# Sparse and latent attention in one decoder layer: the first attention's units taken in a staggered order of row tiles

## The chip, the cores and the metric
The kernel runs on one core of a Trainium2 chip. The metric is the device time of one execution in microseconds (us); the kernel before takes 309.70 us, the median of 3 runs (309.48 to 309.84).

## What is computed
One decoder layer on x (512 tokens, 1024 wide, float32). One input projection feeds two causal attentions of 8 heads each, A and B.

    h = x @ w_in
    A: score = sum over 8 index heads of iw * relu(iq . ik), causal
       each query keeps its 128 best keys; softmax(q . k / 8) over them, times v
       o_a = that * silu(ga)
    B: q, k, v from low-rank latents; rotary part shared by the heads
       o_b = softmax((qn . kn + qp . kp) / sqrt(96), causal) . v * silu(gb)
    out = concat(o_a, o_b) @ w_out
    x = LayerNorm(2**0.25 * x + out)

In A the kernel does not gather keys: a bias tile holds 0 for a chosen key and a very large negative number for another, and the row softmax runs over all the keys that the causal mask leaves.

## The kernel before
**Tiles.** The 512 rows of queries are four row tiles m = 0 to 3 of 128 rows. A row tile m attends to (m+1)*128 keys, so tile 3 works on 512 columns and tile 0 on 128. P is 128, TT is 4, HEADS is 8.

**Stages.** First come seven groups of input projections (L1067), the index scores and the choice of keys beside them on VectorE, then the projections of the latents (L1067 again), then attention A, then attention B with the output projection (L1348) and the layer norm between its units, then the last row tile's output projection and norm.

**Units.** Both attentions are one list of 64 units, 32 for A and 32 for B. A unit is one head of one row tile. `unit(u)` gives for unit u its pass v (v = u // 8), its row tile m = ORDER[v % 4] with ORDER = [3, 2, 1, 0], its head h and its columns N. So A is now worked as 8 units of tile 3, 8 of tile 2, 8 of tile 1 and 8 of tile 0, and B starts again with tile 3.

**One unit of A, across the engines.** Here and below s(u), T(u) and PV(u) are the three parts of unit u on TensorE (PE):

- s(u), `scores`, L1216 and L1219: two products of 128 rows x N columns into one of two score banks. It waits until VectorE has read that bank, that is until the mask of unit u-2 is done (`masked_ready`).
- mask(u), `mask_unit` on VectorE (DVE), L887: adds the bias, scales, writes `probs` (4 buffers) and the row's extreme.
- exp(u), `exp_unit` on ScalarE (ACT), L611: the exponentials in place, and their sum into a column of `row_sum`.
- T(u), `transposes`, L1275: m+1 transposes of 128x128 into one of two banks. It waits for exp(u), and for the copy of unit u-2 out of the same bank.
- copy(u), `copy_probsT` on ACT, L631: the transposed block from that bank into `probsT`.
- PV(u), `outputs`, L1291: m+1 products, each shown in the trace as two instructions, into one half of `ps_o`; pass v uses half v % 2. It waits for copy(u).

**The order by hand.** Each engine's program is written out. PE's iteration u does s(u), then T(u-2) (T_LAG = 2), then PV(u-4) (PV_LAG = 4), then whatever is hung on that iteration. DVE's iteration u does mask(u), ACT's does copy(u-2) and then exp(u). The queues are in order.

    for u in range(NU + PV_LAG):
        if 2 <= u < NU:
            scores(u)
        if 0 <= u - T_LAG < NU:
            transposes(u - T_LAG)
        if u - PV_LAG >= 0:
            outputs(u - PV_LAG)
        if u == PET_AT:
            qpe_transposes()
        ...

**Hung on these iterations** (fixed numbers, not changed): PE transposes 8 blocks of B's rotary queries in iteration 8 (`qpe_transposes`, L1242; PET_AT = 8) and 4 of its rotary key in iteration 14 (L1249). ACT and DVE each copy four parts of the former, one an iteration, in iterations 9 to 12 (`evac_qpeT`, L603 on ACT, L872 on DVE); ACT copies the latter in 15 (L685) and splits one tile of B's values in 20 (L655). In iteration 24 (O_FIRST + T_LAG) the finished output of tile 3 is transposed (`o_transposes`, L1320), in the same pair of banks as the T blocks, and leaves it through ACT (L645) and then DVE (L919); T(24) comes next in that bank. ACT splits three more tiles of values in iterations 32 and 33, DVE takes their low parts in 33, and the output projection of tile 3 starts in iteration 34.

**End of a pass.** `normalise(v)` on DVE (L903, L904) waits until pass v's last PV is done, takes the reciprocals of 8 columns of `row_sum` and scales the output into `o_norm`; `apply_gate(v)` (L913) multiplies by the gate. They stand in DVE's iterations 4 and 5 of the next pass: 12 and 13, 20 and 21, 28 and 29, 36 and 37. PV's first unit of pass v+2 waits for the normalising of pass v.

**Beside A**, GpSimd (POOL) converts the output weights (L444, L448). SyncE starts loading the second half of those weights and others when the last scores of A are done (L351).

Of the kernel before, what the change touches and what calls it, by code (L numbers as in the profile page):

```python
# [8 lines left out]
TT = SEQ // P  # L9
KT = D_MODEL // P  # L10
A_HEADS, A_DIM = 8, 64
A_WIDTH = A_HEADS * A_DIM
# [15 lines left out]
def build(nc, x, xT, positions, freqs, w_in, q_norm_g, w_uq, kv_norm_g, w_ukv, w_out, ln_g, ln_b, out):  # L28
# [37 lines left out]
    ORDER = [3, 2, 1, 0]  # L66
    HEADS = A_HEADS
    NU_A = TT * HEADS
    NU = 2 * NU_A
    NPASS = 2 * TT  # L70
    NPAIR = TT * B_HEADS // 2

    def unit(u):
        v, h = divmod(u, HEADS)
        m = ORDER[v % TT]
        return v, m, h, (m + 1) * P


    O_AFTER = [[NU_A + HEADS * (i + 1) + OT_AT - T_LAG + b for b in range(2)] for i in range(TT - 1)] + [[NU, NU]]
# [98 lines left out]
    def col(n):  # L178
        nonlocal at
        at += n  # L180
        return small[:, at - n:at]
# [5 lines left out]
    neg_max, row_sum, rinv = col(8), col(NU), col(HEADS)  # L187
# [3 lines left out]
    with ExitStack() as ctx:  # L191
# [4 lines left out]
        def sem(name):  # L196
            return ctx.enter_context(nc.semaphore(name))
# [30 lines left out]
        scores_ready, masked_ready, probs_ready = sem("scores_ready"), sem("masked_ready"), sem("probs_ready")  # L228
        transposed, probsT_copied = sem("transposed"), sem("probsT_copied")
        pv_done = sem("pv_done")  # L230
# [4 lines left out]
        o_ps_read, o_ready = sem("o_ps_read"), sem("o_ready")  # L235
# [39 lines left out]
        def wait_tok(eng, g, m):  # L275

            eng.wait_ge(acc_read[m], 2 * (g + 1))
# [204 lines left out]
        def _(act):  # L482
# [125 lines left out]
            def exp_unit(u):  # L608
                N = unit(u)[3]
                act.wait_ge(masked_ready, u + 1)  # L610
                act.activation(probs[:, u % NPROBS, 0:N], probs[:, u % NPROBS, 0:N], ACT.Exp, bias=neg_max[:, u % 8:u % 8 + 1],  # L611
                               scale=-1.0, accum_out=row_sum[:, u:u + 1]).then_inc(probs_ready, 1)

            for first, dst in ((A_QN, qbT), (A_KN, kbT)):
                for p in range(4):
# [50 lines left out]
            for u in range(NU + T_LAG):  # L666
                if u >= T_LAG:
                    copy_probsT(u - T_LAG)
                i, j = divmod(u - NU_A, HEADS)
# [30 lines left out]
        def _(dve):  # L700
# [8 lines left out]
            def after(ins):  # L709
                dve.wait_ge(dve_step, step(ins))  # L710
# [106 lines left out]
            for i in range((TT - 1) * IDX_HEADS):  # L817
                m, h = 1 + i // IDX_HEADS, i % IDX_HEADS
                N = (m + 1) * P
# [39 lines left out]
            for first, dst in ((F_QT, qaT), (F_KT, kaT)):  # L859
                for h in range(A_HEADS):  # L860
                    n, a = first + h // 2, h % 2
# [6 lines left out]
            def evac_qpeT(j):  # L868

                quad, r = divmod(j, 2)  # L870
                dve.wait_ge(acc_ready, A_END + quad + 1)
                ins = V.tensor_copy(qbT[NOPE:B_QK, 4 * quad + 2 + r, :], ps_y[64 + 32 * r:96 + 32 * r, quad])  # L872
                if r == 1:
                    ins.then_inc(acc_read[2 + quad], 1)


            def mask_unit(u):
                v, m, h, N = unit(u)
                a = v < TT
                bias = spans[m - 1] if a and m > 0 else causal[:, SEQ - N:SEQ]  # L880
                scale = (A_DIM if a else B_QK) ** -0.5
                dve.wait_ge(scores_ready, u + 1)
                if u == 0:
                    dve.wait_ge(bias_ready, 1)
                if u >= NPROBS:
                    dve.wait_ge(transposed, slot_of[u - NPROBS] + 1)
                V.tensor_tensor_reduce(out=probs[:, u % NPROBS, 0:N], in0=ps_s[:, u % 2, 0:N], in1=bias, scale=-scale,  # L887
                                       scalar=3.0e38, op0=ALU.add, op1=ALU.min,
                                       accum_out=neg_max[:, u % 8:u % 8 + 1]).then_inc(masked_ready, 1)
# [9 lines left out]

            def normalise(v):  # L900

                dve.wait_ge(pv_done, HEADS * (v + 1))
                after(V.reciprocal(rinv, row_sum[:, HEADS * v:HEADS * (v + 1)]))  # L903
                V.tensor_tensor(o_norm[:, :].rearrange("p (h d) -> p h d", h=HEADS),  # L904
                                ps_o[:, v % 2].rearrange("p (h d) -> p h d", h=HEADS),
                                rinv.unsqueeze(2).broadcast_to([P, HEADS, A_DIM]), ALU.mult).then_inc(o_ps_read, 1)

            def apply_gate(v):
                m = ORDER[v % TT]
                cols = slice(A_WIDTH * (v // TT), A_WIDTH * (v // TT + 1))  # L910
                dve.wait_ge(o_ps_read, v + 1)
                wait_tok(dve, G_GA, m)
                V.tensor_tensor(gate[:, m, cols], o_norm[:, :], gate[:, m, cols], ALU.mult).then_inc(o_ready, 1)  # L913

            def copy_oT_lo(i, b):
                dst = (oT0, oT1)[i % 2]
                dve.wait_ge(oT_hi_ready, 2 * i + b + 1)
                src = ps_pT[:, slot_of[i, b] % 2].rearrange("p (a b) -> p a b", a=4) if b == 0 else obT[:, :, :]
                V.tensor_tensor(dst[:, 1, 4 * b:4 * b + 4, :], src, dst[:, 0, 4 * b:4 * b + 4, :],  # L919
                                ALU.subtract).then_inc(oT_lo_ready, 1)  # L920
# [3 lines left out]
            def probs_low(u):  # L924
                N, w = unit(u)[3], u % 3
                dve.wait_ge(probsT_copied, u + 1)
                V.tensor_tensor(probsT_b[:, w, 1, 0:N], ps_pT[:, slot_of[u] % 2, 0:N], probsT_b[:, w, 0, 0:N],
                                ALU.subtract).then_inc(probsT_lo_ready, 1)

            def vb_low(n):  # L930
                j = VB_ORDER[n]
                dve.wait_ge(vb_hi_ready, n + 1)
                V.tensor_tensor(vb_parts[j][:, :, 1:3], vb[:, j, :].rearrange("p (q a d) -> p q a d", a=2, d=V_DIM),
                                vb_parts[j][:, :, 0:4:3], ALU.subtract).then_inc(vb_lo_dve, 1)
# [9 lines left out]
            def row_sums(v):  # L944

                dve.wait_ge(probs_ready, HEADS * (v + 1))
                if v > TT:
                    dve.wait_ge(gate_scaled, v - TT)
                V.reciprocal(rinv, row_sum[:, HEADS * v:HEADS * (v + 1)]).then_inc(rinv_ready, 1)

            def gate_obT(i):

                n = slot_of[i, 1]
                dve.wait_ge(transposed, n + 1)
                dve.wait_ge(pair_merged, 8 * (i + 1))
                V.tensor_tensor(obT[:, :, :], obT[:, :, :], ps_pT[:, n % 2].rearrange("p (a b) -> p a b", a=4),
                                ALU.mult).then_inc(obT_ready, 1)
# [42 lines left out]
            for u in range(NU):  # L1000
                if u >= 2:
                    mask_unit(u)
                if u - T_LAG >= NU_A:
                    probs_low(u - T_LAG)
                if u == NU_A + 1:
                    vb_low(1)
                    vb_low(2)
                v, j = divmod(u, HEADS)
                i = v - TT
                if 0 < v <= TT and j == PV_LAG:  # L1010
                    normalise(v - 1)
                if 0 < v <= TT and j == PV_LAG + 1:
                    apply_gate(v - 1)
                if v > TT and j == 2:
                    row_sums(v - 1)
                if 0 <= u - PET_AT - 1 < 4:
                    evac_qpeT(u - PET_AT - 1)
                if u == O_FIRST + T_LAG:
                    copy_oT_lo(0, 0)
                if 1 < i and j == OT_AT:  # L1020
                    copy_oT_lo(i - 1, 0)
                if 0 < i and j == OT_AT + 1:
                    gate_obT(i - 1)
                if 0 < i and j == OT_AT + 2:
                    copy_oT_lo(i - 1, 1)
                if u in PAIR_AT:
                    read_pair(PAIR_AT[u])
                if u - 1 in PAIR_AT and PAIR_AT[u - 1] < POOL_PAIRS:
                    merge_pair(V, PAIR_AT[u - 1])
                for t in range(TT - 2):  # L1030
                    for at_u, take in ln_schedule(t):
                        if at_u == u:
                            take()
# [27 lines left out]
        def _(pe):  # L1061
# [133 lines left out]
            for p in range(4):  # L1195
                pe.wait_ge(acc_read[p], seen(A_QN + p))
                for t in range(QL_T):
                    s, cols = (C_UQN + t) % RING, slice(p * P, (p + 1) * P)
# [32 lines left out]
            for p in range(4):  # L1231
                pe.wait_ge(acc_read[p], seen(A_KN + p))
                s, cols = C_UKN % RING, slice(p * P, (p + 1) * P)
# [77 lines left out]
            def o_transposes(i, b):  # L1311

                m = ORDER[i]
                bank = slot(slot_of[i, b])
                if b == 0:
                    pe.wait_ge(o_ready, i + 1)
                else:
                    pe.wait_ge(gate_scaled, i + 1)
                for j in range(4):
                    ins = nc.tensor.transpose(bank[:, j * P:(j + 1) * P], gate[:, m, (4 * b + j) * P:(4 * b + j + 1) * P], ident[:, :])  # L1320
                ins.then_inc(transposed, 1)
# [33 lines left out]
            for u in range(NU + PV_LAG):  # L1355
# [10 lines left out]
                i, j = divmod(u - NU_A, HEADS)  # L1366
# [13 lines left out]
            for b in range(2):  # L1380
                o_transposes(TT - 1, b)
# [6 lines left out]
T_LAG, PV_LAG = 2, 4  # L1388
# [49 lines left out]
```

## Time and profile before
| | |
|---|---|
| median of 3 runs | 309.70 us (309.48 to 309.84) |
| profiled execution, its own time | 309.57 us |
| its span, first to last instruction | 307.7 us |
| mean granted clock of TensorE | 0.995 |
| busy: PE, weight loads, DVE, ACT, POOL | 294.7, 253.4, 235.3, 170.9, 158.7 us |
| attention A, from s(2) to the first scores of B | 176.76 to 214.57 us |
| chain that ended last | PE 87%, DVE 5% |

The page lists for each engine its busy time and its share of the span, and the chain of work that ended last. A matmul is shown from its start to its modelled end, and neighbours overlap, so a part's real cost on PE is read as the distance from its start to the start of the part behind it. The profiled execution's own time is 0.13 us under the median.

### The profile page before, as it was taken

The page shows a single profiled execution, that of the slowest core. Times are in us where ns is not written, and L with a number is a line of the kernel's source. Part 1 is how long each engine was busy: PE and PEld are TensorE (multiplying, and loading weights), DVE is VectorE, ACT ScalarE, POOL GpSimd, SP SyncE. Part 2 cuts the span into 40 slices and gives each one's busy share as a digit, 9 for nine tenths or more (in the row PEclk, how much of TensorE's full clock was granted, in tenths as well). Part 3 has the DMA queues.
Part 4 walks back from the last instruction along what each step waited for, and adds up shares of the span by engine and source line. Part 5 has one row for each costly group of instructions (what it writes and reads, how often), then busy time and mean ns, then how long its engine had stood idle before and what let it go on. Part 6 is the DMA issues. An engine that isn't in the chain of part 4 may idle for free.

```text
span 307.7 us, 5163 instructions
## 1 busy us (share of the span) xinstructions
PE 294.7 (96%) x1646; PEld 253.4 (82%) x1646; DVE 235.3 (76%) x540; ACT 170.9 (56%) x411; POOL 158.7 (52%) x180
## 2 busy tenths in 40 slices
PE   7979999999999999999999999999999999999990
PEld 7969988888888888888889789998677777888890
DVE  1959967888999999996043644855789998987785
ACT  5843274575242262374357787998867885554200
POOL 4869855303999975535326697820492010335211
PEclk9999999999999999999999999999999999999998
DMA  7947442200434532320058333230950000040411
GB/s 253 342 129 207 136 139 71 68 2 0 117 91 136 154 112 78 102 68 2 0 136 205 140 137 117 90 62 8 350 192 0 2 0 3 0 137 2 136 68 68
DMA packets 14777, 31.24 MB, mean 102 GB/s; under 512 B 1728, under 2 KB 4288, under 8 KB 14752
## 3 DMA queue, kind: packets, MB, share of 16 engines
q1 hardware_dynamic: 14192, 30.60, 32.6%
q10 hardware_dynamic: 560, 0.33, 0.4%
q8 instruction: 13, 0.21, 0.3%
q14 instruction: 12, 0.10, 0.1%
HBM read 26.28 MB, written 2.10 MB: 92 GB/s over the span
## 4 chain that ended last, share of the span: by engine, by line
PE 87%; DVE 5%; issue 2%; DMA 2%; ACT 2%; SPq 0%; POOL 0%; DVEq 0%; ACTq 0%; POOLq 0%
PE ps L1067 46%; PE ps L1348 14%; PE ps L1275 6%; PE ps L1225 5%; PE ps L1291 5%; PE ps L1306 3%; PE ps L1216 2%; DMA w_raw<-in_w_in 2%; PE ps L1219 2%; PE ps L1132 1%; DVE x_lo L717 1%; PE ps L1151 1%; PE ps L1320 1%; PE ps L1122 1%; ACT oT L645 1%
## 5 line engine op out<-in xcount | busy, mean ns | idle before, releaser
L403 POOL TENSOR_TENSOR w_lo<-w_raw,w_hi 128x512 fp32r<-128x512 f32 (+3 forms) x62 | 79.3, 1298 | 41.1 <-ACT w_hi L496 41.0
L1067 PE MATMUL ps<-w_hi,x_hi 128*128 128x512 f32 (+2 forms) x220 | 83.2, 378 | 2.9 <-POOL w_lo L403 1.5
L1067 PE MATMUL ps<-w_hi,x_lo 128*128 128x512 f32 (+2 forms) x220 | 82.0, 373 | 0.0
L1067 PE MATMUL ps<-w_lo,x_hi 128*128 128x512 f32 (+2 forms) x220 | 82.0, 373 | 0.0
L496 ACT ACTIVATE w_hi<-w_raw 128x512 fp32r<-128x512 f32 (+3 forms) x62 | 36.2, 591 | 73.3 <-PE ps L1067 72.3
L1067 PEld LDWEIGHTS ps<-w_hi,x_hi 128*128 128x128 f32 x220 | 41.4, 188 | 9.8 <-issue 2.7
L1067 PEld LDWEIGHTS ps<-w_hi,x_lo 128*128 128x128 f32 x220 | 41.3, 188 | 6.5
L1067 PEld LDWEIGHTS ps<-w_lo,x_hi 128*128 128x128 f32 x220 | 41.4, 188 | 5.9
L1348 PE MATMUL ps<-wo_hi,oT 128*128 128x512 f32 (+1 forms) x144 | 44.3, 372 | 0.0
L611 ACT ACTIVATE probs<-probs,small 128x512 f32<-128x512 f32 (+3 forms) x64 | 35.7, 558 | 11.0 <-DVE small L887 10.5
L1275 PE MATMUL ps<-ident,probs 128*128 128x128 f32 x160 | 28.3, 274 | 1.9 <-ACT probs L611 0.9
L1275 PEld LDWEIGHTS ps<-ident,probs 128*128 128x128 f32 x160 | 20.1, 140 | 11.3 <-issue 6.3
L1348 PEld LDWEIGHTS ps<-wo_hi,oT 128*128 128x128 f32 x144 | 25.7, 189 | 3.3
L840 DVE MATCH_REPLACE8 score<-small,score 128x256 f32<-128x256 f32 (+2 forms) x48 | 25.6, 542 | 0.0
L887 DVE CUSTOM_DVE_ANT_0 probs<-ps,score 128x512 f32<-128x512 f32 (+2 forms) x24 | 13.3, 556 | 14.4 <-PE ps L1219 14.4
L837 DVE MAX8 small<-score 128x8 f32<-128x256 f32 (+2 forms) x48 | 23.5, 545 | 0.0
L1225 PE MATMUL ps<-kbT,qbT 96*128 96x512 f32 (+3 forms) x64 | 22.7, 435 | 0.0
L1291 PE MATMUL ps<-va,probsT 128*128 128x64 f32 x160 | 21.4, 264 | 0.0
L1291 PEld LDWEIGHTS ps<-va,probsT 128*128 128x128 f32 x160 | 20.6, 193 | 0.6 <-issue 0.6
L295 POOL TENSOR_TENSOR obT<-half_sum,crossed 64x128 f32<-64x128 f32 x16 | 8.3, 516 | 24.7 <-DVE oT L919 13.7
L887 DVE CUSTOM_DVE_ANT_0 probs<-ps,causal 128x128 f32<-128x128 f32 (+3 forms) x40 | 17.6, 444 | 3.6 <-PE ps L1225 1.6
L631 ACT ACTIVATE probsT_b<-ps 128x512 fp32r<-128x512 f32 (+3 forms) x32 | 13.8, 431 | 8.4 <-PE ps L1275 8.2
(170 smaller groups left out, 557.4 us busy)
## 6 DMA issues: line engine op xcount, KB each, us to landing
w_raw<-in_w_in SPq DMA_DIRECT2D x20, 512.0 KB, 3.6
kaT_swap<-kaT SPq DMA_DIRECT2D x8, 256.0 KB, 3.7
w_raw<-in_w_out SPq DMA_DIRECT2D x4, 512.0 KB, 5.8
wo_early<-in_w_out SPq DMA_DIRECT2D x4, 512.0 KB, 4.2
wo_raw_b<-in_w_out SPq DMA_DIRECT2D x4, 512.0 KB, 5.1
x_res<-in_x SPq DMA_DIRECT2D x4, 512.0 KB, 7.1
w_raw<-in_w_in SPq DMA_DIRECT2D x4, 416.0 KB, 3.7
x_raw<-in_xT SPq DMA_DIRECT2D x3, 512.0 KB, 6.4
```

The costliest lines, as they stand in the source:

```text
L403: pool.tensor_tensor(w_lo[:, s, 0:n], w_raw[:, s, 0:n], w_hi[:, s, 0:n], ALU.subtract).then_inc(w_lo_ready, 1)
L496: act.activation(dst, w_raw[:, s, 0:n], ACT.Copy).then_inc(w_hi_ready, 1)
L611: act.activation(probs[:, u % NPROBS, 0:N], probs[:, u % NPROBS, 0:N], ACT.Exp, bias=neg_max[:, u % 8:u % 8 + 1], scale=-1.0, accum_out=ro ...
L631: act.activation(dst, ps_pT[:, slot_of[u] % 2, 0:N], ACT.Copy).then_inc(probsT_copied, 1)
L837: step(V.max(top8[:, 8 * j:8 * j + 8], sc))
L840: step(V.match_replace(out=sc, in_to_replace=top8[:, 8 * j:8 * j + 8], in_values=sc, imm_value=TAKEN))
L887: V.tensor_tensor_reduce(out=probs[:, u % NPROBS, 0:N], in0=ps_s[:, u % 2, 0:N], in1=bias, scale=-scale, scalar=3.0e38, op0=ALU.add, op1=A ...
L1067: ins = mm(dst, a, b, start=start and j == 0, stop=stop and j == len(pairs) - 1)
L1225: ins = mm(ps_s[:, b, 0:N], qbT[:, h, t], kbT[:, h, 0:N], start=True, stop=True)
L1275: ins = nc.tensor.transpose(bank[:, j * P:(j + 1) * P], probs[:, u % NPROBS, j * P:(j + 1) * P], ident[:, :])
L1291: ins = mm(ps_o[:, v % 2, h * A_DIM:(h + 1) * A_DIM], probsT[:, u % 3, j * P:(j + 1) * P], va[:, j, h * A_DIM:(h + 1) * A_DIM], start=(j = ...
L1348: ins = mm(out_ps(i, b), oT[i % 2][:, o, k, :], w[:, wcols], start=(r == 0), stop=(r == 3 * KT - 1))
```

## The change
Attention A's 32 units come in pairs of two heads, and the pairs of two row tiles alternate. The passes of A are renumbered: pass 0 is tile 3, pass 1 is tile 0, pass 2 is tile 2, pass 3 is tile 1 (ORDER_A = [3, 0, 2, 1]). The row tiles of units 0 to 31 are then

    3 3 3 3 0 0 3 3 0 0 3 3 0 0 2 2 0 0 2 2 1 1 2 2 1 1 2 2 1 1 1 1

The last unit of tile 3 is unit 11, of tile 0 unit 17, of tile 2 unit 27, of tile 1 unit 31. `normalise` and `apply_gate` follow these: DVE's iterations 16 and 17, 22 and 23, 32 and 33, 36 and 37. Each unit's work is what it was; the sum of a row goes to the column of its pass and head. Attention B, all lags, all banks and all that is hung on fixed iterations stay.

```diff
+    ORDER_A = [3, 0, 2, 1]
+    PAIRS_A = [0, 0, 1, 0, 1, 0, 1, 2, 1, 2, 3, 2, 3, 2, 3, 3]
+    UNITS_A = [(v, 2 * PAIRS_A[:i].count(v) + a) for i, v in enumerate(PAIRS_A) for a in range(2)]
+    LAST_A = [UNITS_A.index((v, HEADS - 1)) for v in range(TT)]
+
     def unit(u):
-        v, h = divmod(u, HEADS)
-        m = ORDER[v % TT]
+        v, h = UNITS_A[u] if u < NU_A else divmod(u, HEADS)
+        m = ORDER_A[v] if v < TT else ORDER[v - TT]
         return v, m, h, (m + 1) * P
+
+    def sum_col(u):
+        v, m, h, N = unit(u)
+        return v * HEADS + h
...
-                               scale=-1.0, accum_out=row_sum[:, u:u + 1]).then_inc(probs_ready, 1)
+                               scale=-1.0, accum_out=row_sum[:, sum_col(u):sum_col(u) + 1]).then_inc(probs_ready, 1)
...
-                dve.wait_ge(pv_done, HEADS * (v + 1))
+                dve.wait_ge(pv_done, LAST_A[v] + 1)
...
-                m = ORDER[v % TT]
-                cols = slice(A_WIDTH * (v // TT), A_WIDTH * (v // TT + 1))
+                m = ORDER_A[v]
+                cols = slice(0, A_WIDTH)
...
-                if 0 < v <= TT and j == PV_LAG:
-                    normalise(v - 1)
-                if 0 < v <= TT and j == PV_LAG + 1:
-                    apply_gate(v - 1)
+                for w in range(TT):
+                    if u == LAST_A[w] + 1 + PV_LAG:
+                        normalise(w)
+                    if u == LAST_A[w] + 2 + PV_LAG:
+                        apply_gate(w)
...
-                    pe.wait_ge(o_ready, i + 1)
+                    pe.wait_ge(o_ready, ORDER_A.index(m) + 1)
```

## Rows read from the trace of the kernel before

**Rows 1.** The page, part 4: the chain that ended last, by engine.
```profile
PE 87%; DVE 5%; issue 2%; DMA 2%; ACT 2%; SPq 0%; POOL 0%; DVEq 0%; ACTq 0%; POOLq 0%
```

**Rows 2.** Busy time by stretch: us, then PE, weight loads, DVE, ACT, POOL, clock, DMA, GB/s.
```profile
176.76:214.57 37.81, 37.08 (x307) 35.27 (x306) 21.96 (x74) 32.16 (x95) 21.17 (x25) 1.00 0.26 83
```

**Rows 3.** Timeline of PE: start us, us busy; one iteration of tile 3, one of tile 0.
```profile
182.37 0.48 PE L1216 MATMUL ps<-kaT,qaT 128*128 128x512 f32 x1
...
182.92 0.60 PE L1275 MATMUL ps<-ident,probs 128*128 128x128 f32 x4
183.35 1.00 PE L1291 MATMUL ps<-va,probsT 128*128 128x64 f32 x8
184.16 0.48 PE L1216 MATMUL ps<-kaT,qaT 128*128 128x512 f32 x1
...
212.29 0.31 PE L1216 MATMUL ps<-kaT,qaT 128*128 128x128 f32 x1
...
212.54 0.30 PE L1275 MATMUL ps<-ident,probs 128*128 128x128 f32 x1
212.68 0.33 PE L1291 MATMUL ps<-va,probsT 128*128 128x64 f32 x2
212.82 0.31 PE L1216 MATMUL ps<-kaT,qaT 128*128 128x128 f32 x1
```

**Rows 4.** Timeline of PE: iterations 4, 25, 26 and 31, where it waits.
```profile
178.48 0.47 PE L1216 MATMUL ps<-kaT,qaT 128*128 128x512 f32 x1
179.29 0.63 PE L1275 MATMUL ps<-ident,probs 128*128 128x128 f32 x4
...
180.57 0.48 PE L1216 MATMUL ps<-kaT,qaT 128*128 128x512 f32 x1
...
208.72 0.31 PE L1216 MATMUL ps<-kaT,qaT 128*128 128x128 f32 x1
...
209.58 0.31 PE L1216 MATMUL ps<-kaT,qaT 128*128 128x128 f32 x1
210.44 0.33 PE L1275 MATMUL ps<-ident,probs 128*128 128x128 f32 x1 [0.44 <-DVE oT L919]
...
213.62 0.33 PE L1216 MATMUL ps<-kaT,qaT 128*128 128x128 f32 x1
214.24 0.30 PE L1275 MATMUL ps<-ident,probs 128*128 128x128 f32 x1 [0.18 <-ACT probs L611]
```

**Rows 5.** The chain in order of time: B's rotary queries in iteration 8.
```profile
187.83 0.88 PE ps L1242 x8
```

**Rows 6.** Timeline of ACT: exponentials and copies of tiles 3, 2 and 0.
```profile
178.35 0.72 ACT L611 ACTIVATE probs<-probs,small 128x512 f32<-128x512 f32 x1
...
179.05 0.59 ACT L631 ACTIVATE probsT<-ps 128x512 f32<-128x512 f32 x1
179.53 0.72 ACT L611 ACTIVATE probs<-probs,small 128x512 f32<-128x512 f32 x1
...
183.55 0.60 ACT L631 ACTIVATE probsT<-ps 128x512 f32<-128x512 f32 x1 [0.50 <-PE ps L1275]
...
191.75 0.61 ACT L611 ACTIVATE probs<-probs,small 128x384 f32<-128x384 f32 x1
...
192.47 0.59 ACT L603 ACTIVATE qbT<-ps 32x512 f32<-32x512 f32 x1
...
213.59 0.40 ACT L611 ACTIVATE probs<-probs,small 128x128 f32<-128x128 f32 x1 [0.39 <-DVE small L887]
...
214.00 0.26 ACT L631 ACTIVATE probsT<-ps 128x128 f32<-128x128 f32 x1
```

**Rows 7.** One line's instructions: duration ns min/median/max, first and last start us.
```profile
L913 DVE TENSOR_TENSOR gate<-o_norm,gate x4: 681/688/1126, 196.6 to 226.0; 128x512 f32<-128x512 f32 x4
```

**Rows 8.** Timeline of all engines, 195 to 197 us: POOL and the first gate.
```profile
195.99 1.18 POOL L444 CAST wo_hi<-w_raw 128x512 fp32r<-128x512 f32 x2
...
196.59 1.13 DVE L913 TENSOR_TENSOR gate<-o_norm,gate 128x512 f32<-128x512 f32 x1
```

## The prediction
> **What bounds the kernel now.** I read the chain of waits first: TensorE (PE) carries 87% of it [rows 1], so an edit pays only where PE stands still. Then the stretch of attention A, from s(2) to the first scores of B, because only its order changes: 37.81 us at full clock, ACT busy 32.16, DVE 21.96, POOL 21.17 [rows 2]. ACT is thus the second engine, close behind.
>
> PE's busy time overlaps itself, so I price its work by distances between starts. An iteration of tile 3 takes 1.79 us: 0.55 for s, 0.43 for T, 0.81 for PV. One of tile 0 takes 0.53: 0.25, 0.14, 0.14 [rows 3]. Tiles 2 and 1 I take on the line between: 0.45, 0.33, 0.59 and 0.35, 0.24, 0.36. Where an iteration is longer than its parts, PE waited. There are four such places:
>
> - iteration 4: T(2) starts 0.81 behind s(4) where s takes 0.55, so 0.26, for exp(2) [rows 4];
> - iteration 26: s(26) ends at 209.58 + 0.25 = 209.83 and T(24) starts at 210.44, so 0.61, for the bank that the transposed output of tile 3 leaves through ACT and DVE [rows 4];
> - iteration 30, 212.82 to 213.62, 0.80 where the parts take 0.53: 0.27 [rows 3, 4];
> - iteration 31, 213.62 to B's first scores at 214.57, 0.95: 0.42 [rows 2, 4]. In these last two DVE is normalising and gating the pass before, and the masks of short units stand behind it.
>
> Together 1.56 us. No order of the units can give back more than this in A, since the sum of PE's work is the same in any order.
>
> **The change, part by part.** Removed and added instructions: none. The 32 units keep their products, exponentials and copies; only which unit meets which changes. An iteration then has s(u), T(u-2) and PV(u-4) of different tiles. In the first half the pairs alternate between tile 3 and tile 0, which makes long iterations of 0.55 + 0.14 + 0.81 = 1.50 and short ones of 0.25 + 0.43 + 0.14 = 0.82.
>
> ACT's share evens out less well, because fixed work hangs on iterations 9 to 12. An exponential of tile 3 is followed by a copy after 0.70, and the copy by the next exponential after 0.48; tile 0 takes 0.41 and about 0.17 (0.26 less the overlap of 0.1 that tile 3's copy shows). One of the four extra copies takes 0.60, and the exponential ahead of it 0.11 more than its busy time: 191.75 to 192.47 is 0.72 where the row says 0.61 [rows 6]. So ACT needs 0.48 + 0.51 + 0.60 or 0.17 + 0.83 + 0.60, that is 1.6 us, in each of iterations 9 to 12, and 0.89 in 13: 7.3 us. PE needs 0.82 + 1.50 + 1.50 + 0.82 + 0.82 = 5.46. PE must be held back there unless the lag of two iterations swallows 1.8 us. I step through it:
>
> - Iteration 4: T(2) still waits for exp(2), and s(4) is now 0.25 long. The wait grows to 0.56; s(5) starts at 180.57 as now [rows 4]. After three iterations of 1.5 and iteration 8 with its 0.88 of other transposes [rows 5], 1.70, s(9) starts at 186.7, s(12) at 190.5, s(13) at 191.4.
> - A copy starts 0.63 behind its T (182.92 to 183.55) [rows 3, 6], so copy(7) starts at 187.6. With four blocks of 1.6 exp(11) starts at 191.0, exp(12) at 192.9, and ACT is free at 194.0.
> - T(11) needs exp(11) plus 0.94 (178.35 to 179.29) [rows 4, 6], 191.9, where PE stands at 191.6: wait 0.33. T(12) needs exp(12) plus 0.65 (213.59 to 214.24) [rows 4, 6], 193.56, where PE has come to 192.96: wait 0.60.
> - Then PE goes on with PV(10) and the other transposes: s(15) at 194.9, s(18) at 197.8, and it is ready for T(16) at 198.2. ACT, with its next extra copy in iteration 15, starts exp(16) at 197.8, so T(16) at 198.5: wait 0.27.
> - Iteration 26: the way of the transposed output through ACT and DVE takes 1.72 (208.72 to 210.44) [rows 4]. PE covers it with s(25), T(23), PV(21), s(26) of tiles 1, 2, 1, 2: 0.35 + 0.33 + 0.36 + 0.45 = 1.49, where it now has about 1.1. I put 0.27 for what is left and for an ACT with longer copies.
> - Iterations 28 to 31 are units of tiles 2 and 1, 1.0 us each, and no normalising falls on them: the waits of 0.27 and 0.42 go.
> - Normalising and gating move. Pass 1's fall on iterations 22 and 23, of over 1.2 us each, and cost nothing, as those in 12 and 13 cost nothing now. Pass 0's fall on 16 and 17, of 0.72 us each, the shortest in the list; I cost them at nothing beside the 0.27 above, since ACT is later there than DVE. That is the weakest zero.
> - Pass 2's fall on 32 and 33, beside B's first scores, whose iterations are 0.4 us longer than now because PV(28) to PV(31) are of tile 1 (0.36 against 0.14) and T(30), T(31) too: that is the same work seen later, about 1.1 us, and it covers DVE. What runs behind DVE there has a PE wait only if mask(34) is over 1 us late. Zero.
> - POOL's conversions wait for no unit, so they lose nothing; SyncE's loads behind A's last scores keep their place against B. The reordered sum columns and waits add no instruction.
>
> **The sum.** Waits after: 0.56 + 0.33 + 0.60 + 0.27 + 0.27 = 2.03. Waits before: 1.56. Difference +0.47, onto the profiled execution's own 309.57: **310.0 us**. That execution lies 0.13 under the median of 309.70; against the median the difference is 0.3 to 0.5. Ends of the unknown terms: if the lag swallows all of ACT's excess and only 0.56 and 0.27 remain, 309.57 - 0.73 = 308.8. If nothing of the 1.8 is swallowed instead of half, +0.9, and if the gate in iteration 17 is exposed by 0.45 (below), 311.4. I take the middle because it is the stepped working and because the order of now shows a lag that swallows some, not all: the same four extra copies make ACT blocks of about 1.7 beside PE iterations of 1.35 to 1.7, with no wait.
>
> The Trainium skill, Perfetto Trace Analysis, section Identifying the Most-Contended Engine, judges TensorE's headroom by the busy share of its weight loads, not of its matmuls. Here that is 35.27 of 37.81 us, which leaves 2.54 where my distances leave 1.56 [rows 2]; by it the most the change could bring would be 307.0. I keep the distances, since the first product of tile 3's scores moves 512 columns and its time is longer than the weight load under it.
>
> **Rivals.**
>
> *Interleaving evens the load, faster.* For it: in A's last quarter PE waits for DVE and ACT while in the first it does not, and a mean iteration of a 3-0 pair, 1.16 us, is above ACT's 0.88 without the extra copies. If the ACT queue is then ahead when iteration 9 comes, the waits of T(11), T(12) and T(16) vanish: 308.8. Against it: ACT cannot be ahead, as exp(u) needs s(u) of the same iteration. The same page of the Trainium skill, section Optimization Strategy, advises to interleave stretches with different bounds; it speaks for this case, and by it the gain would be the 0.7 us of this paragraph. A part of the waits gone, 309.2, still counts as faster by half. Chance 0.2.
>
> *Iteration 17's gate locks, slower.* The gate takes 0.69 in three passes and 1.13 in one [rows 7]; that one, at 196.59, ran beside a POOL conversion [rows 8]. The Trainium skill, SBUF - State Buffer, section SBUF: two separate sides, says that a VectorE instruction with two SBUF inputs and a GpSimd one that reads SBUF exclude each other; the trace agrees. Pass 0's gate now falls at about 198.3, between the masks of units 17 and 18 in iterations of 0.72, and POOL still converts there. From the point where mask(18) starts later than 199.2, T(18) waits: up to 0.45. With 0.2 more from a lag that swallows only the 0.7 it does now, 310.7. It decides from 0.28 us over my sum. Chance 0.3, with a sum in which ACT's blocks are longer than 1.6 in it.
>
> *B's start.* Pass 2's normalising and gating (about 1.6 us of DVE) with the low parts of the values push mask(34) and the first low part of the probabilities. If PV(32) waits for it, +0.5: 310.5. Against: the margin counted above. It shares the 0.3.
>
> *The change does not do what it says:* the list holds each pass eight times and each head once, so no. No chance set.
>
> **Numbers.** What a measurement of this kernel can tell from no change is about 0.2%, 0.62 us: 309.08 to 310.32. My sum lies inside, near the upper edge. Faster 0.2, same 0.5, slower 0.3. Range 308.9 to 311.0: it takes in the first rival and most of the second; the likeliest case alone is 309.4 to 310.5.
>
> **What would show it.** In the profile after: B's first scores at about 214.0 (0.6 earlier, with 1.1 us of A's work behind them); T(2) at 179.29 with 0.56 of wait; gaps ahead of T(11) and T(12) put down to ACT's exponentials; none in iterations 28 to 31; weight loads of the stretch unchanged in number. I am wrong if T(12) does not wait (then ACT's queue has slack that I deny), or if a gap opens behind iteration 31.

## The result and the profile after

The changed kernel takes 310.49 us, the median of 17 runs (310.16 to 310.70), beside 309.84 for the kernel before (17 runs, 309.48 to 310.17): ratio 1.0021, 95% interval 1.0014 to 1.0027. It is 0.65 us slower. The forecast was 310.0 with a range of 308.9 to 311.0 and no measurable change as the likeliest case. The time is in the range, but 0.65 lies just beyond the 0.62 that the prediction counted as no change, and the interval is clear of 1: the case that came is "slower", which had a chance of 0.3, and not "same", which had 0.5.

The page of the changed kernel has the same instructions, 1646 matmuls and 5163 in all, and the chain has moved from TensorE to ScalarE and to waits without a releaser ("issue"), as against [rows 1]:

```profile
span 308.7 us, 5163 instructions
...
PE 84%; DVE 5%; ACT 4%; issue 3%; DMA 2%; SPq 0%; POOL 0%; DVEq 0%; ACTq 0%; POOLq 0%
```

The two profiled executions are further apart than the medians, 310.57 against 309.57, and the busy time by stretch says where that microsecond is. The first stretch answers to [rows 2] and runs from s(2) to B's first scores; the second goes on to s(36), from where both kernels' work is alike again; the third is the rest.

```profile
176.69:214.48 37.79, 36.37 (x298) 33.81 (x296) 21.32 (x71) 32.67 (x98) 20.87 (x25) 1.00 0.27 83
176.69:222.00 45.31, 43.89 (x337) 39.05 (x336) 27.32 (x86) 38.88 (x113) 23.11 (x27) 1.00 0.39 128
222.00:308.70 86.70, 78.45 (x449) 65.05 (x447) 72.00 (x182) 43.09 (x127) 25.15 (x32) 0.97 0.16 55
```

In the kernel before, with the same columns:

```profile
176.76:221.02 44.26, 43.53 (x338) 39.43 (x337) 26.02 (x84) 37.89 (x112) 22.35 (x26) 1.00 0.36 120
221.02:307.70 86.68, 78.44 (x449) 65.05 (x447) 72.90 (x184) 43.75 (x128) 26.24 (x33) 0.98 0.18 60
```

The rest takes 86.70 against 86.68. Whatever changed lies between s(2) and s(36), 45.31 against 44.26, and B's first scores are at 214.48 although 1.1 us of A's work now stands behind them. The clock is 1.00 in both. This stretch, from s(2) to s(36), is the measure of every experiment below, since the part ahead of it, alike in all these kernels, varies from execution to execution (s(2) starts at 176.69 to 177.78 in the traces of this study). The stretch can vary too, by 0.4 in three traces of the changed kernel (below), and most kernels have one trace only.

The new waits, on PE's timeline of the changed kernel. T(2), T(11), T(12), T(16), T(18) and T(24), each below the s that is ahead of it:

```profile
178.41 0.31 PE L1226 MATMUL ps<-kaT,qaT 128*128 128x128 f32 x1
...
179.23 0.63 PE L1285 MATMUL ps<-ident,probs 128*128 128x128 f32 x4 [0.40 <-ACT probs L620]
...
191.32 0.30 PE L1226 MATMUL ps<-kaT,qaT 128*128 128x128 f32 x1
...
191.90 0.63 PE L1285 MATMUL ps<-ident,probs 128*128 128x128 f32 x4 [0.17 <-ACT probs L620]
...
192.51 0.42 PE L1226 MATMUL ps<-kaT,qaT 128*128 128x384 f32 x1
...
193.50 0.30 PE L1285 MATMUL ps<-ident,probs 128*128 128x128 f32 x1 [0.40 <-ACT probs L620]
...
197.69 0.42 PE L1226 MATMUL ps<-kaT,qaT 128*128 128x384 f32 x1
...
198.43 0.30 PE L1285 MATMUL ps<-ident,probs 128*128 128x128 f32 x1
...
200.35 0.36 PE L1226 MATMUL ps<-kaT,qaT 128*128 128x256 f32 x1
...
201.04 0.52 PE L1285 MATMUL ps<-ident,probs 128*128 128x128 f32 x3 [0.21 <-ACT probs L620]
...
207.36 0.42 PE L1226 MATMUL ps<-kaT,qaT 128*128 128x384 f32 x1
...
208.06 0.44 PE L1285 MATMUL ps<-ident,probs 128*128 128x128 f32 x2
```

From the start of s to that of T is 0.25, 0.43 or 0.32 where nothing waits (tiles 0, 2, 1). Here it is 0.82, 0.58, 0.99, 0.74, 0.69 and 0.70: waits of 0.57, 0.33, 0.56, 0.31, 0.37 and 0.27. The brackets name ScalarE's exponential. T(16) and T(24) have none; T(16) stands behind exp(16) (an experiment below), and T(24), as in the kernel before, behind the bank that the transposed output of tile 3 leaves. A bracket shows less than the whole wait or nothing, since a matmul's modelled end covers part of it: read the distances, not the brackets.

ScalarE in the same stretch, from copy(7) to exp(12):

```profile
187.57 0.60 ACT L640 ACTIVATE probsT<-ps 128x512 f32<-128x512 f32 x1 [0.71 <-PE ps L1285]
188.06 0.39 ACT L620 ACTIVATE probs<-probs,small 128x128 f32<-128x128 f32 x1
...
188.57 0.58 ACT L612 ACTIVATE qbT<-ps 32x512 f32<-32x512 f32 x1
189.17 0.28 ACT L640 ACTIVATE probsT<-ps 128x128 f32<-128x128 f32 x1
189.34 0.71 ACT L620 ACTIVATE probs<-probs,small 128x512 f32<-128x512 f32 x1
...
190.96 0.71 ACT L620 ACTIVATE probs<-probs,small 128x512 f32<-128x512 f32 x1
...
192.38 0.60 ACT L640 ACTIVATE probsT<-ps 128x512 f32<-128x512 f32 x1
192.88 0.39 ACT L620 ACTIVATE probs<-probs,small 128x128 f32<-128x128 f32 x1
```

It never pauses between these: 1.6 us an iteration, with one extra copy (L612) in each, while PE has iterations of 0.86 among its long ones.

### The profile page after: what moved, and what is told of

Read it like the earlier page. It is cut to its first block, busy times and chain, and to the rows that moved or that the text cites. A ratio compares the mean times of both kernels' runs of the same rounds, so it can differ in the third digit from the quotient of the medians.

```text
span 308.7 us, 5163 instructions
## 1 busy us (share of the span) xinstructions
PE 294.6 (95%) x1646; PEld 252.7 (82%) x1646; DVE 235.4 (76%) x540; ACT 171.3 (55%) x411; POOL 159.0 (52%) x180
## 4 chain that ended last, share of the span: by engine, by line
PE 84%; DVE 5%; ACT 4%; issue 3%; DMA 2%; SPq 0%; POOL 0%; DVEq 0%; ACTq 0%; POOLq 0%
PE ps L1077 46%; PE ps L1358 14%; PE ps L1285 5%; PE ps L1235 5%; PE ps L1301 4%; PE ps L1316 3%; DMA w_raw<-in_w_in 2%; DVE x_lo L726 1%; PE ps L1142 1%; ACT probs L620 1%; PE ps L1226 1%; PE ps L1161 1%; PE ps L1229 1%; PE ps L1330 1%; PE ps L1132 1%
```

## The experiments

All experiments compute what the kernel computes; each but the repeats moves some of the hand-placed work, or changes the list of units. Times are medians of 11 runs, 6 for the first one with copies moved, and one run for each repeat, beside 21 or 28 of the kernel before on the same chip. The changed kernel has no such median beside them, so each time is set against the kernel before, and the changed kernel's 0.65 is that of the result above. "Stretch" is s(2) to s(36) in one trace.

### The gate of pass 0 moved off GpSimd's conversions

```diff
-                    if u == LAST_A[w] + 2 + PV_LAG:
+                    if u == (21 if w == 0 else LAST_A[w] + 2 + PV_LAG):
```

> The changed kernel with one edit: pass 0's gate moves from VectorE's iteration 17 to 21, when GpSimd has no conversion left. Theory (the gate held by GpSimd delays mask(18) and so T(18)): the gate takes 0.69 us instead of 1.77, the wait of 0.37 us ahead of T(18) is gone, and the time is 0.3 to 0.4 us under the changed kernel's, that is 0.2 to 0.35 over the kernel before. Rival (ScalarE is late there anyway, or the gate is as long wherever it stands): the wait ahead of T(18) stays over 0.25 us and the time stays 0.65 over the kernel before.

310.50 against 309.79, ratio 1.0022 (1.0013 to 1.0031): 0.71 over the kernel before, so no gain over the changed kernel's 0.65. Yet its trace shows what the theory said: the gate takes 0.69 us, the wait ahead of T(18) is gone, 0.32 from the start of s(20), and the stretch is 0.31 shorter than in the changed kernel's trace:

```profile
200.50 0.36 PE L1226 MATMUL ps<-kaT,qaT 128*128 128x256 f32 x1
...
200.82 0.49 PE L1285 MATMUL ps<-ident,probs 128*128 128x128 f32 x3
```

By the columns of [rows 2]:

```profile
176.75:221.75 45.00, 43.78 (x338) 39.03 (x336) 26.30 (x86) 39.07 (x113) 22.68 (x27) 1.00 0.39 127
```

So one trace of the changed kernel has a wait that this one lacks, and the medians show no gain. Whether the wait was the kernel's or that one execution's, more traces of the changed kernel can tell.

### The changed kernel traced again, twice

> The changed kernel itself once more, for its trace. Theory (how much of pass 0's gate GpSimd holds up depends on when the loads that its conversions wait for land, which differs from run to run): the gate takes another time than the 1.77 us of the first trace, between 0.69 and 1.8, and the wait ahead of T(18) goes with it: none below 1.2 us of gate. Rival (the 1.77 belongs to this order): 1.7 to 1.8 again, with 0.37 of wait.

> As the run before it: a third trace of the changed kernel, with the same two expectations.

310.60 and 310.81 us, one run each. The gate took 0.97 and 0.99 us, both T(18) waited for nothing (0.32 behind s(20)), and the stretches are 44.91 and 44.90, which is 0.65 and 0.64 over the kernel before:

```profile
177.14:222.05 44.91, 43.70 (x338) 39.02 (x337) 26.61 (x86) 39.05 (x113) 23.09 (x27) 1.00 0.40 129
```

That is the difference of the medians. It can't be read from single executions as a whole: the three of the changed kernel took 310.57, 310.60 and 310.81, the shortest with the longest stretch, as its s(2) started earliest (176.69, 177.14, 177.36). VectorE and GpSimd on the timelines, first of the first trace, then of the first repeat:

```profile
197.86 2.96 POOL L457 TENSOR_TENSOR wo_lo_a<-w_raw,wo_hi 128x512 fp32r<-128x512 f32 x2
...
197.91 1.77 DVE L922 TENSOR_TENSOR gate<-o_norm,gate 128x512 f32<-128x512 f32 x1
```

```profile
197.50 2.97 POOL L457 TENSOR_TENSOR wo_lo_a<-w_raw,wo_hi 128x512 fp32r<-128x512 f32 x2
...
198.36 0.97 DVE L922 TENSOR_TENSOR gate<-o_norm,gate 128x512 f32<-128x512 f32 x1
```

What differs is when GpSimd's last pair of subtractions starts against the gate: 0.05 us ahead of it in the first trace, 0.86 in the repeat. Ahead of that GpSimd waited for two loads, 2.47 and 1.43 us in the first trace, 2.95 and 0.17 in the repeat. The profile of after happened to catch a bad meeting: 0.4 of its 1.05 us are not in the other two traces. The repeats also say that the trace of the experiment above shows nothing of its edit, since T(18) waits for nothing in them without it.

### Two of ScalarE's extra copies moved back

```diff
-                if 0 <= u - PET_AT - 1 < 4:
-                    evac_qpeT(u - PET_AT - 1)
+                if u in (9, 10, 14, 19):
+                    evac_qpeT((9, 10, 14, 19).index(u))
```

> The changed kernel with one edit: of ScalarE's four extra copies of rotary queries, in iterations 9 to 12, the last two go to iterations 14 and 19. Theory (these copies beside short iterations make exp(11) and exp(12) late): the waits ahead of T(11) and T(12), 0.33 and 0.55 us, fall under 0.1 together, T(16)'s stays near 0.3 and T(18)'s near 0.4; the time is 0.7 to 0.9 under the changed kernel's, 0.05 to 0.25 under the kernel before. Rival (it is the alternation of long and short units that makes them late, whatever the copies): both waits stay over 0.2 and the time gains under 0.3.

310.59 against 309.79, ratio 1.0029 (1.0017 to 1.0040), stretch 45.02: both expectations missed in part. T(12) no longer waits. T(11) does, by the same 0.33, and I should have seen it: exp(11) stands behind the copies of 9 and 10 alone, which had not moved. And a new wait of 0.56 stands ahead of T(20), where the copy of iteration 19 makes exp(20) late; ScalarE splits a value tile right behind it, in iteration 20. First T(11), then T(20):

```profile
192.27 0.63 PE L1285 MATMUL ps<-ident,probs 128*128 128x128 f32 x4 [0.17 <-ACT probs L620]
...
202.80 0.41 PE L1285 MATMUL ps<-ident,probs 128*128 128x128 f32 x2 [0.40 <-ACT probs L620]
```

### Both edits together

> The changed kernel with both edits, the gate in iteration 21 and the two copies in 14 and 19. Theory (the two costs are separate): 1.1 to 1.3 us under the changed kernel's time, 0.45 to 0.65 under the kernel before; waits left in attention A about 1.2 us: T(2) 0.57, T(24) 0.27, T(16) up to 0.3. Rival (one cost hides behind the other, so that removing both gives little more than one): not over 0.9 under the changed kernel's.

310.52 against 309.79, ratio 1.0024 (1.0015 to 1.0033), stretch 44.93, no better than one edit alone: the wait of 0.57 ahead of T(20) is there again. The theory's 1.1 to 1.3 fell with the misplaced copy.

### The copies moved to where ScalarE has room

The changed kernel with the four copies, and not the gate, moved: as above with (9, 12, 27, 29).

> The changed kernel with one edit: ScalarE's four extra copies stand in iterations 9, 12, 27 and 29 instead of 9 to 12, so that none is ahead of exp(10) and exp(11), one ahead of exp(13), and the last two beside iterations of 1.0 to 1.2 us. Theory (the first spread gained nothing because the copy in 19 made exp(20) late, beside the split of a value tile in 20; the copies must stand where ScalarE has room): the waits ahead of T(11) and T(12) are both gone and no new one over 0.1 us appears, the time is 0.7 to 1.0 us under the changed kernel's, 0.05 to 0.3 under the kernel before. Rival (ScalarE has no room anywhere in this order, so a wait removed comes back somewhere): within 0.3 of the changed kernel.

309.82 against 309.86, ratio 1.0000 (0.9991 to 1.0009), so the changed kernel's 0.65 are gone. T(11) and T(12) wait for nothing, 0.25 and 0.44 behind their s:

```profile
191.81 0.30 PE L1226 MATMUL ps<-kaT,qaT 128*128 128x128 f32 x1
...
192.06 0.62 PE L1285 MATMUL ps<-ident,probs 128*128 128x128 f32 x4
...
192.66 0.42 PE L1226 MATMUL ps<-kaT,qaT 128*128 128x384 f32 x1
...
193.10 0.27 PE L1285 MATMUL ps<-ident,probs 128*128 128x128 f32 x1
```

T(28) waits 0.11, and the stretch is that of the kernel before to 0.02:

```profile
177.18:221.42 44.24, 43.59 (x337) 39.08 (x336) 26.36 (x86) 38.99 (x113) 23.11 (x27) 1.00 0.40 130
```

So the loss of the changed kernel is that ScalarE's extra copies meet short iterations. The other new waits, 0.3 more ahead of T(2) and 0.31 ahead of T(16), are still there; with the small ones they use up what the end of attention A gives back. The time equals the kernel before's; 0.05 to 0.3 under it were expected, and 0.11 of the difference came back in iteration 30, ahead of T(28).

### The rotary key's copy moved too

```diff
-                if u == PET_AT + 7:
+                if u == 26:
```

> The kernel with ScalarE's four copies in 9, 12, 27 and 29, and now its copy of the rotary key too, from iteration 15 to 26. Theory (T(16)'s wait of 0.31 us and PV(14)'s 0.1 behind it are that copy's, ahead of copy(14) and exp(16)): both fall under 0.1 together, the time is 0.3 to 0.45 under the kernel before. Rival (VectorE's normalising in iteration 16 makes them): the wait stays over 0.25 and the time within 0.15 of the kernel before.

309.90 against 309.91, ratio 1.0000 (0.9991 to 1.0009), stretch 44.39. The wait ahead of T(16) and the 0.1 behind it are gone (iteration 18 takes 1.21 us, before it 1.62), so they were this copy's and not the normalising's. But with copies in 26, 27 and 29 the waits come back one after the other there, 0.56 ahead of T(28):

```profile
212.64 0.41 PE L1285 MATMUL ps<-ident,probs 128*128 128x128 f32 x2 [0.40 <-ACT probs L620]
```

The time expected (0.3 to 0.45 under the kernel before) did not come. The rival of the run before, that a wait removed comes back elsewhere, is half right: in this placement of the five extra copies it does. No other placement was tried.

### Pass 2's normalising and gate moved, in the order of before

```diff
-                if 0 < v <= TT and j == PV_LAG:
-                    normalise(v - 1)
-                if 0 < v <= TT and j == PV_LAG + 1:
-                    apply_gate(v - 1)
+                if u in (12, 20, 32, 36):
+                    normalise((12, 20, 32, 36).index(u))
+                if u in (13, 21, 33, 37):
+                    apply_gate((13, 21, 33, 37).index(u))
```

> The kernel before, its order of units kept, with one edit: pass 2's normalising and gate on VectorE move from iterations 28 and 29 to 32 and 33, where the staggered order has them. Theory (the waits of 0.27 and 0.42 us in iterations 30 and 31 come from masks that stand behind them on VectorE): both go, and the time is 0.4 to 0.7 under the kernel before. Rival (short units in a row wait for ScalarE and VectorE in any case, and only an order without such a run helps): at least half of the 0.69 stays, the time is within 0.3.

309.32 against 309.86, ratio 0.9985 (0.9976 to 0.9993): 0.54 faster, stretch 43.78. Iterations 30 and 31 fall from 0.80 and 0.95 to 0.65 and 0.64. The starts of s(30), s(31) and B's first scores, then the stretch by the columns of [rows 2]:

```profile
213.12 0.31 PE L1216 MATMUL ps<-kaT,qaT 128*128 128x128 f32 x1
...
213.77 0.31 PE L1216 MATMUL ps<-kaT,qaT 128*128 128x128 f32 x1
...
214.41 1.10 PE L1225 MATMUL ps<-kbT,qbT 96*128 96x512 f32 x2
```

```profile
177.07:220.85 43.78, 43.23 (x338) 39.33 (x336) 25.82 (x84) 37.77 (x111) 22.45 (x26) 1.00 0.37 117
```

Two thirds of the 0.69 that these iterations waited (0.46) were the masks behind the normalising and the gate, and no staggering is needed to get them.

### The same, with tile 3's output transposed earlier

```diff
-O_FIRST = 22
+O_FIRST = 19
```

> The order of before with pass 2's normalising in 32, and the transposes of tile 3's output three iterations earlier, in 21 instead of 24, where the units around are of tile 1. Theory (the wait ahead of T(24), 0.61 us, is the way of that block through ScalarE and VectorE, and longer units cover more of it): the wait falls to 0.3 to 0.5 and the time is 0.6 to 0.9 under the kernel before. Rival (POOL's conversions, which must be done first, end only near 201.5 us, and the block gets through no earlier): no gain over the 0.54 measured without this edit.

309.48 against 309.91, ratio 0.9984 (0.9975 to 0.9993), stretch 43.81: no gain over the edit before. The wait moved from T(24) to T(21) and shrank to 0.50, and 0.2 turned up in the iteration behind it. The rival's number came, but not its reason (GpSimd ends too late): the block's way from the start of the next s to the T behind it takes 1.72 (206.34 to 208.06), as long as in 24.

### Another list: long units under the copies, no run of short ones at the end

```diff
-    ORDER_A = [3, 0, 2, 1]
-    PAIRS_A = [0, 0, 1, 0, 1, 0, 1, 2, 1, 2, 3, 2, 3, 2, 3, 3]
+    ORDER_A = [3, 2, 0, 1]
+    PAIRS_A = [0, 0, 0, 0, 1, 1, 1, 2, 1, 2, 3, 3, 2, 3, 2, 3]
```

> The changed kernel with another list of units and nothing else: pairs of tiles 3 3 3 3 2 2 2 0 2 0 1 1 0 1 0 1, so that iterations 9 to 12 with the extra copies have long units only, and short ones stand between longer ones at the end. Theory (what costs is short units beside ScalarE's extra copies, what gains is that no run of short units stands ahead of attention B): T(2)'s wait is back at 0.26, nothing waits in iterations 9 to 14, and the sum of waits in attention A is about 0.6 to 0.9 us against 1.56 before: 308.7 to 309.3, that is 0.5 to 1.1 under the kernel before. Rival (alternating tiles of unlike length costs as much as it gives, wherever it stands): within 0.3 of the kernel before.

309.25 against 309.79, ratio 0.9982 (0.9973 to 0.9991), 0.54 faster, the low end of what was expected. Iterations 9 to 13 are those of the kernel before and wait for nothing; the stretch is 0.58 shorter, and the wait ahead of T(24) is about 0.4 where it was 0.61. First s(26) and T(24) on PE's timeline, then the stretch by the columns of [rows 2]:

```profile
208.52 0.36 PE L1226 MATMUL ps<-kaT,qaT 128*128 128x256 f32 x1
...
209.26 0.33 PE L1285 MATMUL ps<-ident,probs 128*128 128x128 f32 x1 [0.26 <-DVE oT L928]
```

```profile
176.94:220.62 43.68, 43.30 (x337) 39.27 (x336) 25.41 (x82) 38.44 (x112) 22.73 (x27) 1.00 0.37 127
```

This list and the moved normalising (with its variant above) are the versions that beat both kernels, and the times of the two can't be told apart. They are not two separate ideas: pass 2's last unit is unit 29 in this list, so its normalising and gate stand in VectorE's iterations 34 and 35, behind A's masks, as in the experiment above they stand in 32 and 33. Such a move alone gave 0.54. No run has this list with the normalising left among the short units, or takes the two effects apart in another way, so how much of the 0.54 the interleaving itself gives is not shown.

## Why the prediction was right where it was, and where not

**The bound** held: PE is busy 294.6 us where it was 294.7, and the difference is one of waits. The sum of PE's waits went from 1.56 to about 2.2 us in the typical trace.

**T(2)**: forecast 0.56, measured 0.57. **T(11)** 0.33 and 0.33, **T(12)** 0.60 and 0.56, with exp(11) and exp(12) forecast at 191.0 and 192.9 and found at 190.96 and 192.88. The blocks of 1.6 us on ScalarE were right, and the run with the copies moved late shows that they are the cause.

**T(16)**: 0.27 and 0.31, by the cause named, the copy of iteration 15. What I left out is that PV(14) waits another 0.07 right behind it.

**Iteration 26**: 0.27 and 0.27. **Iterations 28 to 31**: no waits, as forecast. The part "no normalising falls on them: the waits of 0.27 and 0.42 go" was right about the cause for two thirds; the last third stays in the order of before when the normalising is moved, and is gone in the changed one, whose last units are longer. Of these iterations only 28 and 29 take the 1.0 that I gave to all four; 30 and 31 take 1.13 and 1.16, as PV(26) and PV(27) are of tile 2, and nothing waits in them.

**The weakest zero**, normalising and gating in iterations 16 and 17, was indeed one: in one trace of three the gate took 1.77 us, more than the 1.13 that I had as its bound, and T(18) waited 0.37, within the 0.45 of the rival. In the other two traces the zero held. The Trainium skill, SBUF - State Buffer, section SBUF: two separate sides, has the two engines exclude each other for whole instructions, whichever starts first. The first trace agrees (last section): GpSimd's instruction that began ahead of the gate kept its length, and the gate and the instruction behind it were stretched.

**B's start**: zero. PE goes through iterations 32 to 35 at 1.52, 1.53, 2.26, 2.21, each longer than before by what its longer T or PV adds (0.30, 0.34, 0.21, 0.22; the 0.4 of the prediction was too much). B's first scores were forecast 0.6 earlier against s(2); they come 0.43 and 0.44 earlier in the repeats, and 0.02 in the first trace with its long gate.

**The size.** The sum was +0.47 and the repeated traces give +0.65. The missing 0.18 is two terms that I didn't have: the 0.07 of PV(14), and 0.11 in iteration 23, which takes 1.36 us where s(23), T(21) and PV(19) take 1.25. On the timeline T(21) comes behind exp(21), which ScalarE starts only after the split of a value tile in iteration 20 (202.48, 0.62 us) and copy(19): one more piece of fixed work beside shortened iterations. No run moves this split, so that it is the cause is read from the order and not tested. The mechanism was right and, in the two traces without the long gate, each term that was in the sum was within 0.04 us. The forecast of 310.0 was further set on an execution of 309.57, which lies 0.27 under the median of 309.84 that more runs gave; taken from that median, the same +0.47 would have been 310.3.

**The rivals.** "Interleaving evens the load" was wrong for this list. The other list, which also alternates, is 0.54 faster, so alternation as such does not decide the loss; the copies beside short units do. That it evens the load for a gain is open, since that list takes the normalising out of the way as well. "Iteration 17's gate locks" was real in one trace of three; how often it comes, the traces don't say. It is not the reason for the 0.65, which the two traces without it show in full.

**The headroom.** The Trainium skill, Perfetto Trace Analysis, section Identifying the Most-Contended Engine, would have allowed 2.54 us by the busy time of the weight loads. The best list saved 0.58 of the stretch, so neither this nor the 1.56 of the distances was reached; whether PE could gain the 0.98 by which the two measures differ, no run shows.

## What to carry to other kernels

Before units of unlike length are interleaved, list what else is hung on fixed iterations of each engine: fixed work that a long iteration hides is a wait beside a short one. Add up, for each engine and each iteration, what it has to do until the result is needed, and compare running sums and not the averages of the stage (ScalarE's average of 32 us in 38 looked roomy, and over five iterations it had, by the prediction's sums, 7.3 us of work beside 5.5 of PE's). When a wait has one identifiable cause, such as a normalising queued ahead of masks, move that cause first; here it gave as much as the best reordering. And ask of a reordering what else it moves along, before its gain is put down to the order.

## What the runs showed of the hardware

A VectorE multiply of two SBUF tiles (128x512) took 0.69 us alone and between 0.69 and 1.77 us beside GpSimd's instructions on SBUF. In the first trace of the changed kernel GpSimd's pair of subtractions starts 0.05 us ahead of the gate. The first of the pair takes 1.28 us, its usual time, and the gate 1.77; the second begins at 199.1, while the gate runs, and takes 1.73:

```profile
L457 POOL TENSOR_TENSOR wo_lo_a<-w_raw,wo_hi x2: 1275/1502/1729, 197.9 to 199.1; 128x512 fp32r<-128x512 f32 x2
```

GpSimd can also be the one that pays. With the gate short at 0.71 us, a pair of casts that takes 1.17 us elsewhere took 1.63; the timelines of the kernel with the copies in 9, 12, 27 and 29 show it:

```profile
193.13 1.17 POOL L453 CAST wo_hi<-wo_early 128x512 fp32r<-128x512 f32 x2 [2.25 <-DMA wo_early<-in_w_out]
197.04 1.63 POOL L453 CAST wo_hi<-wo_early 128x512 fp32r<-128x512 f32 x2 [2.74 <-DMA wo_early<-in_w_out]
...
197.48 0.71 DVE L922 TENSOR_TENSOR gate<-o_norm,gate 128x512 f32<-128x512 f32 x1
```

Which of the two pays depends on some tenths of a microsecond, and so a single profile can show a wait that other executions of the same kernel don't have.
